# Attention of a hybrid decoder layer: straight-line code, four relayout transfers in place of sixteen, and q loaded ahead of them

## The chip, the cores and the metric

One core of one Trainium2 chip runs the whole kernel. The time is device microseconds (us) of one execution, and less is better. Besides the timed runs there is one profiled execution, with its own time and its own span (from its first to its last instruction).

## The reference

One hybrid layer on 2048 tokens of width 1024. A projection makes q, k, v, a gate and the inputs of a state-space scan; the attention merges three dilated patterns (window 128 step 1, window 512 step 4, window 2048 step 16), normalised by their common denominator, and is gated; the state-space branch is scanned in chunks; both go through one output projection.

```python
u = rms_norm(hid, norm_pre_w)
proj = jnp.einsum('bsd,de->bse', u, w_in)
q, k, v, g_attn, z, xbc, dt_raw = jnp.split(proj, ...)
attn = mixture_of_dilations(q * 64 ** -0.5, k, v)    # 16 heads of 64, 3 patterns, merged by denominators
attn = attn * silu(g_attn)
...                                                   # conv, ssd_chunked, gated group norm: y
out = jnp.einsum('bse,ed->bsd', concat([attn, y]), w_out)
return hid + rms_norm(out, norm_post_w)
```

## The kernel before, in words

The kernel has three blocks in a row: `project` (to about 1260 us), `attend` (to about 1923 us) and `scan_and_project` (to the end). The change touches `attend` alone.

**Work of a head.** The tokens fall into 4 classes by their number modulo 4. A head is 32 units. Units 0 to 15 are "class" units: unit s holds the queries of class c = s % 4 in block n = s // 4, against blocks 0 to n of the same class (this covers the patterns with steps 4 and 16). Units 16 to 31 are "natural" units: 128 tokens in a row against the block before and their own. Two heads are a pair, and the 64 units of a pair are the steps p of one `body`.

**Order of a unit, written out by hand.** TensorE (PE) makes the scores (L1104, L1105: high and rest part of k) three steps ahead; VectorE (DVE) adds the mask and takes the row minimum (L935, from PSUM to `masked`); ScalarE (ACT) exponentiates (L1051); PE transposes the probabilities (L1112); DVE, or at every fourth unit ACT, copies them out (L981, L1087); PE multiplies them with v (L1125) two steps later; ACT reads a group of 8 units out of PSUM (L1063) into `cls_out` (class units) or `nat_out` (natural ones). The rings are four `masked`, `probs` and `probs_t` buffers, three score banks and two banks of transposes, so a stop of one engine reaches the others within a few units.

**Between heads.** `cls_out` of a head has a class unit's 128 queries on the partitions, so SyncE (SP) moves it by DMA into natural order, `cls_nat` (`relayout`, L751: 16 transfers a head, each 32 partitions of source and 4 units of 66 numbers). At unit 3 of the next head DVE takes the common minimum (`merge_drops`, L946, L949), ACT the weights, DVE at unit 5 the denominators and scales (`merge_scales`, L957 to L965). GpSimd (POOL) multiplies and adds the two parts (`merge`, L717, L722); PE transposes a finished pair at units 16, 20, 24 and 28 of an even head (L1136), and DVE gates it. For the last head DVE does the merge too.

**Loads.** SP's queue runs, for head h (`load_head`): wait until head h-2 is weighed with v; 4 + 4 transfers of v for head h (L761, L764); the relayout of head h-1, after a wait for its class groups; then q and k of head h+1 (`load_qk`, L739, two transfers each, after waits that the buffers `raw_q` and `raw_k` are free, which POOL signals with its steps L702 and L704 on head h); for every second head the gate g. Of q and k of the next head ACT takes the high parts at units 5, 7, 9, 11 (q) and 13 to 19 (k), L1030; POOL takes the rests (L702, L704) and sorts q by class (L709). The first score of the next head, made at unit 29, waits for all of it.

**Loops.** On every engine pair 0 and pair 7 are written out and pairs 1 to 6 are one hardware loop, so each engine branches back five times:

```python
            body(0)
            with eng.Fori(1, HEADS // 2 - 1) as pair:
                body(pair)
            body(HEADS // 2 - 1)
```

Of the kernel before, what the change touches and what calls it, by code (L numbers as in the profile page):

```python
# [14 lines left out]
P = 128  # L15
# [496 lines left out]
def attend(nc, dram, dt_bias, a_log, cum_tok, dt_tok):  # L512
# [5 lines left out]
    with ExitStack() as ctx:  # L518
# [25 lines left out]
        cls_out = [sb(f"cls_out{b}", [P, CLASS_UNITS, WIDE]) for b in range(2)]  # L544
        cls_nat = [sb(f"cls_nat{b}", [P, TT, WIDE]) for b in range(2)]
# [36 lines left out]
        pool_waited = sem("pool_waited")  # L582
# [19 lines left out]
        dve_waited = sem("dve_waited")  # L602
# [11 lines left out]
        class Unit:  # L614


            def __init__(self, p):
                self.b, self.s = divmod(p, UNITS)
                self.group = self.s // GROUP
                if self.s < CLASS_UNITS:  # L620
# [6 lines left out]
                    self.min = cls_out[self.b][:, self.s, HEAD_DIM + 1:HEAD_DIM + 2]  # L627
                    self.sum = cls_out[self.b][:, self.s, HEAD_DIM:HEAD_DIM + 1]
# [23 lines left out]
        def loop_pairs(eng, body):  # L652


            body(0)
            with eng.Fori(1, HEADS // 2 - 1) as pair:
                body(pair)
            body(HEADS // 2 - 1)
# [52 lines left out]

        def merge(eng, head, b):
# [3 lines left out]
            for j, (dst, src) in enumerate(((part_a, nat_out[b][:, :, :]), (part_b, cls_nat[b][:, :, 0:HEAD_DIM]))):  # L716
                eng.tensor_tensor(dst[:, :, :], src, scale[:, j, :].unsqueeze(2).broadcast_to([P, TT, HEAD_DIM]),  # L717
                                  ALU.mult).then_inc(merge_part, 1)
# [8 lines left out]
        with nc.Block() as block:  # L727
            @block.sync
            def _(sp):
# [4 lines left out]
                def load_qk(head):  # L734

                    for x, at in (("q", 0), ("k", D_ATTN)):
                        wait(sp, split[x], head)
# [4 lines left out]
                def relayout(head, b):  # L742
# [6 lines left out]
                    for c in range(CLASSES):  # L749
                        for j in range(CLASSES):  # L750
                            sp.dma_start(cls_nat[b][c:P:CLASSES, j:TT:CLASSES, :],  # L751
                                         cls_out[b][j * rows:(j + 1) * rows, c:CLASS_UNITS:CLASSES, :])\
                              .then_inc(relaid, 16)

                def load_head(head, b, is_last=False):
# [7 lines left out]
                    for c in range(CLASSES):  # L763
                        sp.dma_start(v_nat[b][c * SHARE:(c + 1) * SHARE, :, :], v_natural[c][:, :, cols])\  # L764
                          .then_inc(v_in[b], 16)
                    if not is_int(head, 0):
                        relayout(head - 1, 1 - b)
                    if not is_last:
                        load_qk(head + 1)
# [11 lines left out]
                with sp.Fori(1, HEADS // 2 - 1) as pair:  # L781
# [13 lines left out]
            def _(pool):  # L795
# [23 lines left out]
                def head_turn(head, b, has_before=True, has_next=True):  # L819
# [3 lines left out]
                    if has_next:  # L823
# [5 lines left out]
                        for x in "qk":  # L829
                            pool.wait_ge(high_made[x], (head + 2) * TB)  # L830
                            take_rest(pool, x, 1 - b)
                            if x == "q":
                                pool.wait_ge(split[x], head + 2)
                                pool.sem_inc(pool_waited, 1)
# [919 lines left out]
```

## Time and profile before

| what | value |
|---|---|
| median of 3 runs | 2480.7 us |
| lowest and highest run | 2478.7 and 2482.16 us |
| the profiled execution, its own time | 2473.88 us |
| its span | 2472.2 us |
| busy share of the span: PE, PE weight loads, DVE, ACT, POOL | 93%, 80%, 43%, 34%, 29% |
| mean granted TensorE clock (share of full speed) | 0.963 |
| relayout transfers | 256 of 33.0 KB, median 2.0 us from issue to landing |
| transfers of q, and of k | 32 and 32 of 512.0 KB, median 6.2 and 9.6 us |

PE is TensorE's multiplications, PEld its weight loads, SPq the DMA issues of SyncE. In a row of the time line come the start, the duration, the engine, the line, the operation with the tiles it writes and reads, and in brackets the idle time of the engine just before the row and what ended it; "issue" there means that the engine waited for nothing the profile shows. Two heads take about 80 us in the middle of the attention.

### The profile page before, as it was taken

The numbers are of one execution on the slowest core, as the hardware profiler recorded it, in microseconds if no ns is written. First come the engines' busy times: TensorE is split into PE (matmuls) and PEld (weight loads), VectorE is DVE, ScalarE is ACT, GpSimd is POOL, SyncE is SP. The second block draws the span as 40 slices with busy tenths as digits, with TensorE's granted clock in tenths as the row PEclk, the third lists the DMA queues.
The fourth block names the chain that finished last, engine by engine and source line by source line (L and its number), as shares of the span: only waits on it lengthen the run. The fifth ranks groups of instructions, "written<-read, shape, count | busy, mean of one in ns | idle before, by whom it ended". The sixth has DMA issues, their size and how long they took to land. (4 is left out here: it accounts for less than half of the span.)

```text
span 2472.2 us, 36119 instructions
## 1 busy us (share of the span) xinstructions
PE 2306.9 (93%) x12565; PEld 1972.9 (80%) x12565; DVE 1052.8 (43%) x2245; ACT 832.4 (34%) x2013; POOL 709.7 (29%) x348
## 2 busy tenths in 40 slices
PE   6899999999999999999958998998898499999998
PEld 5788888888888888888848988898898278888886
DVE  4200000011111223465556766666577576666661
ACT  5211111111111111221236766676676332222222
POOL 0011111010011100111105544453553345555552
PEclk9999999999999999999979998998999589999999
DMA  4222221121322122122363635544462724444431
GB/s 129 93 77 77 77 76 60 52 76 51 94 76 60 52 76 77 51 76 68 95 123 83 152 79 136 137 113 100 112 151 56 281 94 140 139 139 132 134 109 52
DMA packets 270854, 244.47 MB, mean 99 GB/s; under 512 B 112677, under 2 KB 245985, under 8 KB 259073
## 3 DMA queue, kind: packets, MB, share of 16 engines
q1 hardware_dynamic: 269632, 235.56, 34.3%
q0 software_dynamic: 1104, 7.47, 0.8%
q8 instruction: 58, 0.95, 0.2%
q14 instruction: 60, 0.48, 0.1%
HBM read 160.67 MB, written 73.66 MB: 95 GB/s over the span
## 5 line engine op out<-in xcount | busy, mean ns | idle before, releaser
L442 PE MATMUL mm<-u_hi,w_hi 128*128 128x512 f32 x1696 | 666.4, 393 | 16.2 <-DVE u_lo L371 14.2
L444 PE MATMUL mm<-u_hi,w_lo 128*128 128x512 f32 x1696 | 662.6, 391 | 0.0
L443 PE MATMUL mm<-u_lo,w_hi 128*128 128x512 f32 x1696 | 662.6, 391 | 0.0
L254 POOL TENSOR_TENSOR w_lo<-w_raw,w_hi 128x1024 fp32r<-128x1024 f32 x53 | 139.5, 2632 | 1089.7 <-ACT w_hi L268 1089.7
L442 PEld LDWEIGHTS mm<-u_hi,w_hi 128*128 128x128 f32 x1696 | 320.0, 189 | 84.1 <-DVE u_lo L371 17.3
L444 PEld LDWEIGHTS mm<-u_hi,w_lo 128*128 128x128 f32 x1696 | 319.8, 189 | 66.9
L443 PEld LDWEIGHTS mm<-u_lo,w_hi 128*128 128x128 f32 x1696 | 320.3, 189 | 65.5
L417 DVE COPY tok_tile<-turn 128x512 f32<-128x512 f32 x104 | 64.6, 683 | 578.7 <-PE turn L457 576.5
L1112 PE MATMUL ps_t<-ident_b,probs 128*128 128x128 f32 x1136 | 222.0, 286 | 52.7 <-DVE probs_t L981 38.9
L1639 PE MATMUL ps_out<-wo_hi,mix_hi 128*128 128x512 f32 x512 | 208.0, 406 | 1.3 <-ACT mix_hi L1588 1.3
L1112 PEld LDWEIGHTS ps_t<-ident_b,probs 128*128 128x128 f32 x1136 | 141.6, 145 | 78.6 <-DVE probs_t L981 33.7
L1640 PE MATMUL ps_out<-wo_lo,mix_hi 128*128 128x512 f32 x512 | 200.6, 392 | 0.0
L1125 PE MATMUL ps_o<-v_cls,probs_t 128*128 128x64 f32 x1280 | 182.8, 276 | 0.0
L981 DVE COPY probs_t<-ps_t 128x256 f32<-128x256 f32 (+3 forms) x384 | 171.9, 448 | 22.6 <-issue 19.6
L1125 PEld LDWEIGHTS ps_o<-v_cls,probs_t 128*128 128x128 f32 x1280 | 175.7, 204 | 0.8 <-issue 0.7
L386 DVE SCALAR_TENSOR_TENSOR fm<-half_tanh,mm 128x512 f32<-128x512 f32 x64 | 44.0, 688 | 297.4 <-ACT half_tanh L293 297.4
L935 DVE CUSTOM_DVE_ANT_0 masked<-ps_s,class_mask 128x128 f32<-128x128 f32 (+3 forms) x256 | 124.2, 490 | 91.0 <-PE ps_s L1105 33.9
L1051 ACT ACTIVATE probs<-masked,cls_out 128x128 f32<-128x128 f32 (+3 forms) x256 | 141.7, 556 | 39.0 <-DVE cls_out L935 38.7
L935 DVE CUSTOM_DVE_ANT_0 masked<-ps_s,near_mask 128x256 f32<-128x256 f32 (+1 forms) x256 | 106.3, 415 | 89.6 <-PE ps_s L1105 70.3
L293 ACT ACTIVATE half_tanh<-mm 128x512 f32<-128x512 f32 x64 | 38.2, 597 | 307.2 <-PE mm L444 307.2
L1125 PE MATMUL ps_o<-v_nat,probs_t 128*128 128x64 f32 x992 | 138.7, 261 | 0.0
L1051 ACT ACTIVATE probs<-masked,nat_min 128x256 f32<-128x256 f32 (+1 forms) x256 | 126.3, 497 | 18.5 <-DVE nat_min L935 18.4
(181 smaller groups left out, 3434.0 us busy)
## 6 DMA issues: line engine op xcount, KB each, us to landing
feat<-fm SPq DMA_DIRECT2D x28, 1024.0 KB, 4.7
w_raw<-in_w_in_dram SPq DMA_DIRECT2D x52, 512.0 KB, 6.2
tok<-tok_tile SPq DMA_DIRECT2D x26, 1024.0 KB, 5.6
raw_q<-feat SPq DMA_DIRECT2D x32, 512.0 KB, 6.2
raw_k<-feat SPq DMA_DIRECT2D x32, 512.0 KB, 9.6
cum_b<-cum_scratch SPq DMA_DIRECT2D x16, 1024.0 KB, 7.6
cls_nat<-cls_out SPq DMA_DIRECT2D x256, 33.0 KB, 2.0
tok_tile<-in_x_dram SPq DMA_DIRECT2D x16, 512.0 KB, 3.6
```

The costliest lines, as they stand in the source:

```text
L254: pool.tensor_tensor(w_lo[b][:, :, :], w_raw[b][:, :, :], w_hi[b][:, :, :].bitcast(F32), ALU.subtract).then_inc(w_lo_made[b], 1)
L417: dve.tensor_copy(tok[:, q * 4:q * 4 + 4, :].rearrange("p a b -> p (a b)"), turn[q][:, :])\
L442: pe.matmul(mm[tb][:, :], w_hi[b][:, k, :], u_hi[:, k, block_cols(tb)], start=(k == 0), stop=False)
L443: pe.matmul(mm[tb][:, :], w_hi[b][:, k, :], u_lo[:, k, block_cols(tb)], start=False, stop=False)
L444: last = pe.matmul(mm[tb][:, :], w_lo[b][:, k, :], u_hi[:, k, block_cols(tb)], start=False, stop=(k == KT - 1))
L935: dve.tensor_tensor_reduce(out=masked[p % RING][:, 0:u.width], in0=ps_s[p % S_BANKS][:, 0:u.width], in1=u.mask, scale=1.0, scalar=3e38, op ...
L981: copy_probs(dve, pair, p, lambda o, i: dve.tensor_copy(o, i))
L1051: act.activation(probs[p % RING][:, 0:u.width], masked[p % RING][:, 0:u.width], ACT.Exp, bias=u.min, scale=-1.0, accum_out=u.sum).then_inc ...
L1112: last = pe.transpose(ps_t[p % 2][:, j * P:(j + 1) * P], probs[p % RING][:, j * P:(j + 1) * P], ident[:, :])
L1125: last = pe.matmul(ps_o[u.group % 2][:, (u.s % GROUP) * HEAD_DIM:(u.s % GROUP + 1) * HEAD_DIM], probs_t[p % RING][:, j * P:(j + 1) * P], u ...
L1639: pe.matmul(ps_out[h][:, :], mix_hi[:, kk, :], wo_hi[:, kk, cols_h], start=(kk == 0), stop=False)
L1640: pe.matmul(ps_out[h][:, :], mix_hi[:, kk, :], wo_lo[:, kk, cols_h], start=False, stop=False)
```

## The change

`attend` is written out: `loop_pairs` calls the body for each of the 8 pairs, and the loops of SP and POOL become Python loops too. Semaphore values and addresses become constants, and two counters that nothing waits for (`dve_waited`, `pool_waited`) go. `cls_out` and `cls_nat` are kept as [class, block, 66], so the 4 blocks of a class lie side by side in a partition, and `relayout` is 4 transfers a head of 1056 bytes for each of 128 destination partitions; before it was 16 with pieces of 264 bytes. The readers and writers of the two tiles get other access patterns. In SP's queue q of head h+1 is loaded ahead of the relayout of head h-1, k behind it as before.

```diff
         count, near = masked[2], masked[3]
-        cls_out = [sb(f"cls_out{b}", [P, CLASS_UNITS, WIDE]) for b in range(2)]
-        cls_nat = [sb(f"cls_nat{b}", [P, TT, WIDE]) for b in range(2)]
+        cls_out = [sb(f"cls_out{b}", [P, CLASSES, CLASS_BLOCKS, WIDE]) for b in range(2)]
+        cls_nat = [sb(f"cls_nat{b}", [P, CLASSES, CLASS_BLOCKS, WIDE]) for b in range(2)]
         nat_out = [sb(f"nat_out{b}", [P, TT, HEAD_DIM]) for b in range(2)]
...
                     self.v = [v_cls[self.b][:, c * CLASS_BLOCKS + j, :] for j in range(self.blocks)]
-                    self.min = cls_out[self.b][:, self.s, HEAD_DIM + 1:HEAD_DIM + 2]
-                    self.sum = cls_out[self.b][:, self.s, HEAD_DIM:HEAD_DIM + 1]
+                    self.min = cls_out[self.b][:, c, n, HEAD_DIM + 1:HEAD_DIM + 2]
+                    self.sum = cls_out[self.b][:, c, n, HEAD_DIM:HEAD_DIM + 1]
                 else:
...
-        def loop_pairs(eng, body):
-
-
-            body(0)
-            with eng.Fori(1, HEADS // 2 - 1) as pair:
+        def loop_pairs(body):
+
+
+            for pair in range(HEADS // 2):
                 body(pair)
-            body(HEADS // 2 - 1)
...
+        def by_row(ap):
+
+            return ap.rearrange("p (n j) -> p n j", j=CLASSES)
+
+        def in_order(ap):
+
+            return ap.rearrange("p j n -> p n j")
+
         def merge(eng, head, b):
...
             wait(eng, merge_part, head * 3)
-            for j, (dst, src) in enumerate(((part_a, nat_out[b][:, :, :]), (part_b, cls_nat[b][:, :, 0:HEAD_DIM]))):
-                eng.tensor_tensor(dst[:, :, :], src, scale[:, j, :].unsqueeze(2).broadcast_to([P, TT, HEAD_DIM]),
-                                  ALU.mult).then_inc(merge_part, 1)
+            eng.tensor_tensor(part_a[:, :, :], nat_out[b][:, :, :],
+                              scale[:, 0, :].unsqueeze(2).broadcast_to([P, TT, HEAD_DIM]), ALU.mult).then_inc(merge_part, 1)
+            eng.tensor_tensor(part_b[:, :, :].rearrange("p (n j) f -> p n j f", j=CLASSES),
+                              cls_nat[b][:, :, :, 0:HEAD_DIM].rearrange("p j n f -> p n j f"),
+                              by_row(scale[:, 1, :]).unsqueeze(3).broadcast_to([P, CLASS_BLOCKS, CLASSES, HEAD_DIM]),
+                              ALU.mult).then_inc(merge_part, 1)
             eng.wait_ge(merge_part, head * 3 + 2)
...
-                def load_qk(head):
+                def load_qk(head, which="qk"):
                     for x, at in (("q", 0), ("k", D_ATTN)):
+                        if x not in which:
+                            continue
                         wait(sp, split[x], head)
...
                     rows = P // CLASSES
-                    for c in range(CLASSES):
-                        for j in range(CLASSES):
-                            sp.dma_start(cls_nat[b][c:P:CLASSES, j:TT:CLASSES, :],
-                                         cls_out[b][j * rows:(j + 1) * rows, c:CLASS_UNITS:CLASSES, :])\
-                              .then_inc(relaid, 16)
+                    for j in range(CLASSES):
+                        sp.dma_start(cls_nat[b][:, j, :, :].rearrange("p n f -> p (n f)"),
+                                     cls_out[b][j * rows:(j + 1) * rows, :, :, :].rearrange("p c n f -> p c (n f)"))\
+                          .then_inc(relaid, 16)
...
                           .then_inc(v_in[b], 16)
+                    if not is_last:
+                        load_qk(head + 1, "q")
                     if not is_int(head, 0):
...
                     if not is_last:
-                        load_qk(head + 1)
+                        load_qk(head + 1, "k")
                     if b == 1:
...
                 load_head(1, 1)
-                with sp.Fori(1, HEADS // 2 - 1) as pair:
+                for pair in range(1, HEADS // 2 - 1):
                     load_head(pair * 2, 0)
...
                 head_turn(1, 1)
-                with pool.Fori(1, HEADS // 2 - 1) as pair:
+                for pair in range(1, HEADS // 2 - 1):
                     head_turn(pair * 2, 0)
...
                         wait(dve, scales_made, pair * 2 + u.b - 1)
-                    dve.sem_inc(dve_waited, 1)
                     dve.tensor_tensor_reduce(out=masked[p % RING][:, 0:u.width], in0=ps_s[p % S_BANKS][:, 0:u.width],
...
-                    mins = [nat_min[b][:, :], cls_nat[b][:, :, HEAD_DIM + 1]]
+                    mins = [nat_min[b][:, :], in_order(cls_nat[b][:, :, :, HEAD_DIM + 1])]
                     at = head * 9
-                    dve.wait_ge(relaid, (head + 1) * CLASSES * CLASSES * 16)
+                    dve.wait_ge(relaid, (head + 1) * CLASSES * 16)
                     dve.wait_ge(group_out, head * 4 + 4)
                     dve.wait_ge(exped, head * UNITS + UNITS)
-                    dve.tensor_tensor(both_min[:, :], mins[0], mins[1], ALU.min).then_inc(merge_step, 1)
+                    dve.tensor_tensor(by_row(both_min[:, :]), by_row(mins[0]), mins[1], ALU.min).then_inc(merge_step, 1)
                     dve.wait_ge(merge_step, at + 1)
                     for j in range(2):
-                        dve.tensor_tensor(drop[:, j, :], mins[j], both_min[:, :], ALU.subtract).then_inc(merge_step, 1)
+                        dve.tensor_tensor(by_row(drop[:, j, :]), by_row(mins[j]) if j == 0 else mins[j],
+                                          by_row(both_min[:, :]), ALU.subtract).then_inc(merge_step, 1)
...
-                    sums = [nat_sum[b][:, :], cls_nat[b][:, :, HEAD_DIM]]
+                    sums = [nat_sum[b][:, :], in_order(cls_nat[b][:, :, :, HEAD_DIM])]
                     at = head * 9
...
                     for j in range(2):
-                        dve.tensor_tensor(part_sum[:, j, :], sums[j], weight[:, j, :], ALU.mult).then_inc(merge_step, 1)
+                        dve.tensor_tensor(by_row(part_sum[:, j, :]), by_row(sums[j]) if j == 0 else sums[j],
+                                          by_row(weight[:, j, :]), ALU.mult).then_inc(merge_step, 1)
                     dve.wait_ge(merge_step, at + 5)
...
-                loop_pairs(dve, body)
+                loop_pairs(body)
                 merge_drops(HEADS - 1, 1)
...
                     at = (u.group % 2) * GROUP
-                    dst = (cls_out[u.b][:, at:at + GROUP, 0:HEAD_DIM] if u.s < CLASS_UNITS
-                           else nat_out[u.b][:, at:at + GROUP, :])
+                    if u.s < CLASS_UNITS:
+                        rows = slice(at // CLASSES, (at + GROUP) // CLASSES)
+                        dst = cls_out[u.b][:, :, rows, 0:HEAD_DIM].rearrange("p c n f -> p n c f")
+                        src = ps_o[u.group % 2][:, :].rearrange("p (n c f) -> p n c f", c=CLASSES, f=HEAD_DIM)
+                    else:
+                        dst = nat_out[u.b][:, at:at + GROUP, :]
+                        src = ps_o[u.group % 2][:, :].rearrange("p (u f) -> p u f", f=HEAD_DIM)
                     if u.group == 2:
                         wait(act, merge_part, (pair * 2 + u.b - 1) * 3)
-                    act.activation(dst, ps_o[u.group % 2][:, :].rearrange("p (u f) -> p u f", f=HEAD_DIM), ACT.Copy)\
-                       .then_inc(group_out, 1)
+                    act.activation(dst, src, ACT.Copy).then_inc(group_out, 1)
...
-                loop_pairs(act, body)
+                loop_pairs(body)
                 group_read(HEADS // 2 - 1, STEPS - 1)
...
                 pe.wait_ge(made, 7)
-                loop_pairs(pe, body)
+                loop_pairs(body)
                 for p in range(STEPS - 2, STEPS):
```

## Rows read from the trace of the kernel before

**Rows 1.** Waits, 1334 to 1911 us: total, times, longest (us)

```profile
PE ps_t L1112 <- DVE probs_t L981: 30.5, 10, 4.3
...
DVE masked L935 <- issue: 24.3, 7, 5.2
...
DVE probs_t L981 <- issue: 19.6, 5, 4.5
```

**Rows 2.** Time line of DVE: first step of the merge, at unit 3

```profile
1334.25 0.18 DVE L946 TENSOR_TENSOR both_min<-nat_min,cls_nat 128x16 f32<-128x16 f32 x1
...
1370.04 0.18 DVE L946 TENSOR_TENSOR both_min<-nat_min,cls_nat 128x16 f32<-128x16 f32 x1
...
1406.64 0.17 DVE L946 TENSOR_TENSOR both_min<-nat_min,cls_nat 128x16 f32<-128x16 f32 x1
...
1808.19 0.18 DVE L946 TENSOR_TENSOR both_min<-nat_min,cls_nat 128x16 f32<-128x16 f32 x1
...
1842.48 0.18 DVE L946 TENSOR_TENSOR both_min<-nat_min,cls_nat 128x16 f32<-128x16 f32 x1
...
1879.14 0.18 DVE L946 TENSOR_TENSOR both_min<-nat_min,cls_nat 128x16 f32<-128x16 f32 x1
```

**Rows 3.** Time line of DVE at one backward branch

```profile
1521.74 0.29 DVE L935 CUSTOM_DVE_ANT_0 masked<-ps_s,class_mask 128x128 f32<-128x128 f32 x1 [5.23 <-issue]
...
1529.32 0.42 DVE L981 COPY probs_t<-ps_t 128x256 f32<-128x256 f32 x1 [3.69 <-issue]
```

**Rows 4.** Windows of 10 us: busy (instructions) of PE, PEld, DVE, ACT, POOL; clock; DMA share

```profile
1410.00:1420.00 10.00, 9.59 (x77) 9.03 (x78) 7.77 (x24) 8.89 (x25) 9.36 (x4) 1.00 1.11 316
...
1520.00:1530.00 10.00, 5.79 (x23) 5.02 (x24) 3.62 (x18) 3.99 (x14) 0.00 (x0) 0.62 0.99 194
...
1530.00:1540.00 10.00, 10.00 (x56) 9.20 (x55) 6.54 (x25) 6.20 (x17) 6.13 (x3) 0.70 0.20 41
```

**Rows 5.** DMA queues of kind instruction, 1366 to 1438 us: packets, MB

```profile
q8 instruction: 5, 0.08, 0.5%
...
q14 instruction: 6, 0.05, 0.3%
```

**Rows 6.** Time line of PE: idle after the wait for q

```profile
1338.96 0.44 PE L1112 MATMUL ps_t<-ident_b,probs 128*128 128x128 f32 x2 [1.77 <-ACT probs L1051]
...
1374.32 0.44 PE L1112 MATMUL ps_t<-ident_b,probs 128*128 128x128 f32 x2 [1.34 <-ACT probs L1051]
...
1811.51 0.44 PE L1112 MATMUL ps_t<-ident_b,probs 128*128 128x128 f32 x2 [0.31 <-ACT probs L1051]
...
1846.96 0.44 PE L1112 MATMUL ps_t<-ident_b,probs 128*128 128x128 f32 x2 [1.56 <-ACT probs L1051]
```

**Rows 7.** Time line of ACT: the wait for q ahead of one of them

```profile
1373.15 0.63 ACT L1030 ACTIVATE q_parts<-raw_q 128x512 fp32r<-128x512 f32 x1 [1.85 <-DMA raw_q<-feat]
```

**Rows 8.** Time line of SP's DMA issues ahead of it

```profile
1355.14 10.49 SPq L751 DMA_DIRECT2D cls_nat<-cls_out  x16
...
1365.91 1.20 SPq L739 DMA_DIRECT2D raw_q<-feat  x2
```

**Rows 9.** Time line of POOL in the same stretch

```profile
1345.40 4.54 POOL L702 TENSOR_TENSOR q_parts<-raw_q,q_parts 64x2048 fp32r<-64x2048 f32 x1 [1.50 <-ACT q_parts L1030]
...
1356.19 4.54 POOL L704 TENSOR_TENSOR k_rest<-raw_k,k_high 128x2048 fp32r<-128x2048 f32 x1 [2.12 <-ACT k_high L1030]
```

**Rows 10.** Groups by form, 1334 to 1911 us: merge and group read

```profile
L717 POOL TENSOR_TENSOR part_b<-cls_nat,scale 128x1024 f32<-128x1024 f32 x15 | 28.5, 1902 | 0.0
...
L717 POOL TENSOR_TENSOR part_a<-nat_out,scale 128x1024 f32<-128x1024 f32 x15 | 28.5, 1898 | 186.8 <-DVEq L967 186.8
...
L1063 ACT ACTIVATE cls_out<-ps_o 128x512 f32<-128x512 f32 x30 | 17.8, 595 | 0.0
```

**Rows 11.** Time line at the last merge: DVE

```profile
1911.11 0.19 DVE L946 TENSOR_TENSOR both_min<-nat_min,cls_nat 128x16 f32<-128x16 f32 x1 [2.41 <-DMA cls_nat<-cls_out]
```

**Rows 12.** The same stretch: ACT, the last group read

```profile
1909.57 0.60 ACT L1063 ACTIVATE nat_out<-ps_o 128x512 f32<-128x512 f32 x1 [1.52 <-PE ps_o L1125]
```

More of the change, by code:

```diff
@@ L581, in attend @@
         q_sorted = sem("q_sorted")
-        pool_waited = sem("pool_waited")
         v_in = [sem(f"v_in{b}") for b in range(2)]
@@ L601, in attend @@
         last_out = sem("last_out")
-        dve_waited = sem("dve_waited")
         dt_in = sem("dt_in")
@@ L833, in head_turn @@
                                 pool.wait_ge(split[x], head + 2)
-                                pool.sem_inc(pool_waited, 1)
                                 sort_q(pool, 1 - b)
```

## The prediction, made before the changed kernel was run

> **What bounds the kernel now.** I read the waits of the attention stretch first, then the time line of DVE and of PE, then windows of 10 us. PE is busy nearly all the time in this kernel, so what counts is where PE stands still or runs at a lower clock. Between 1334 and 1911 us PE has one large wait, for DVE's copy of the probabilities: 30.5 us in ten times [rows 1]. DVE itself was then waiting for nothing but its instructions: 24.3 us ahead of the mask and 19.6 us ahead of the copy. Ten of these twelve waits come in pairs, one pair at each of the five backward branches; the other two are 0.2 and 0.5 us. One such place: 5.23 us before the mask, and 7.6 us later 3.69 us before the copy [rows 3]. The windows show what comes with it: 23 and then 56 multiplications in 10 us instead of the 77 of an undisturbed busy stretch, and a granted clock of 0.62 and 0.70, that is part of the time at the lower of its two levels, after PE had been idle; elsewhere it is 1.00 [rows 4].
>
> To price it I use a landmark: DVE's first step of the merge, at unit 3 of each head [rows 2]. Between two of them lies one head. Intervals without a branch are 35.79 and 34.29 us (the work of an odd head), and 36.60 and 36.66 us (an even head, with the 16 transposes of a finished pair). Each has one more idle time of PE, of 1.77, 0.31, 1.34 and 1.56 us [rows 6]: ACT waits at unit 5 for q of the next head, 1.85 us in the second of them [rows 7], and so falls behind with the exponentials. Taken off, the clean heads are 34.02 and 33.98, 35.26 and 35.10 us: 34.0 + 35.2 = **69.2 us for a pair**. That written-out and looped heads agree within 0.2 us says that register arithmetic and the counters cost nothing; it is only the branch.
>
> **The change, part by part.**
>
> (a) The five backward branches go. From the landmark at 1406.64 to that at 1808.19 are 401.55 us for ten heads with all five branches [rows 2]. Clean they are 5 x 69.2 = 346.0. The difference is **55.5 us**: 30.5 us of PE's idle time [rows 1], the rest the low clock behind it and the waits for q of these heads. It is all on the path, since PE is. A price for written-out code in its place: the first pass through the loop, 1366 to 1438 us, had to bring in its instructions like any written-out code, 5 and 6 transfers on the two instruction queues [rows 5], and DVE shows no wait of more than 0.2 us for them there. The transfers of other data do not hold them up either: from 1410 to 1420 us the DMA share is 1.11 and PE is 9.59 of 10 us busy at full clock [rows 4]. So I take 0, with 5.5 us (55.5 / 10) per transfer as the upper end, which is what an exposed one costs today.
>
> (b) q ahead of the relayout. Before: SP issues sixteen relayout transfers from 1355.14 on, q at 1365.91 [rows 8], and q has landed at 1373.15 [rows 7], 7.2 us later. The new order adds a wait of SP, for the buffer of q, ahead of the relayout, k and g. It ends when POOL has taken the rest of q, at 1345.40 + 4.54 = 1349.9 [rows 9]; the relayout was released only at 1355.1, so it is not held up. q lands at about 1357.2, and ACT wants it at 1373.15 - 1.85 = 1371.3: the wait goes, with 14 us to spare. Outside the branches this gives 1.77 + 1.34 + 0.31 + 1.56 = **5.0 us** [rows 6]; the waits inside the branch stretch are in (a) already. Next in line behind q is nothing large: k needs its buffer, free at 1356.19 + 4.54 = 1360.7 [rows 9], and is then issued 6 us earlier than before (1367.3), for use some units later than q. The v transfers that follow keep their own wait (the head before last weighed) and start where they did.
>
> (c) The relayout, 4 for 16. An issue cost SP 10.49 / 16 = 0.66 us for 33 KB, and 0.60 us for half of raw_q with 512 KB [rows 8], so the time goes by the transfer and not by its bytes: 4 x 0.66 = 2.6 us instead of 10.5. Upper end: unchanged 10.5. For fifteen heads it is hidden, since the merge that reads `cls_nat` comes at unit 3 of the next head. After the last head it is not: DVE waited 2.41 us for the last transfer, until 1911.11 [rows 11]. That wait goes, but the same instruction also waits for the last group read of ACT, which ends at 1909.57 + 0.60 = 1910.2 [rows 12]. So the gain is **0.9 us**, not 2.4; lower end 0.
>
> (d) Access patterns. POOL's product takes 1.902 us from `cls_nat` with its gaps and 1.898 us from `nat_out` without any [rows 10]: steps cost nothing there. With one dimension more I take the same; twice as long would be 1.9 us a head, against the 2.12 us that POOL waits for ACT before the rest of k [rows 9], so it is covered. ACT's group read is 0.595 us [rows 10]; twice that for two groups a head would be 1.2 us and up to 19 us over 16 heads if none were covered. I take 0, because its output went already in rows of 64 with gaps of 2 between them. DVE's small merge steps are 0.18 to 0.19 us [rows 11]; 0 as well.
>
> **Sum.** 55.5 + 5.0 + 0.9 = 61.4 us. Against the profiled execution's own 2473.9 us that is 2412.5 us. The median of the runs is 6.8 us above that execution, and nothing in the change touches this difference: 2480.7 - 61.4 = **2419.3 us**, which I forecast.
>
> **The rivals.**
>
> *Only the first wait of each pair goes* (the second, ahead of the copy, stays in some form). For it: it comes 7.6 us behind the branch, not at its target. Then 19.6 / (23.7 + 19.6) = 45% of the 55.5 us stays, 25 us: 2444 us. Against it: no such wait stands in any written-out stretch or in the loop's first pass, which ran the same instructions in the same place. Chance 0.05. The Trainium skill, page "Runtime: NRT & Kernel Launch", section "Instruction fetch mechanics", says that fetching runs ahead sequentially, that crossing to the next block is mostly hidden and that a taken branch breaks it. By that rule the first wait is the fetch and the second would need another cause, which is this rival. The trace agrees with the rule on the first and speaks against it on the second, 3.69 us.
>
> *The early q gives nothing*: ACT's stop at unit 5 has another cause, or q's buffer is not free in time. Mean of the four idle times is 1.25 us, in 14 heads 17.4 us: 2437 us. For it: 1.34 us of idle PE is less than the 1.85 us of the wait, so PE's idle time need not follow it one for one. Against: 14 us of slack. Chance 0.08.
>
> *The waits are not the branch's* but come from the load on the DMA queues at that moment (share 0.99 in the window [rows 4]), so the written-out code has them too; then only q and the end gain: 2480.7 - 18.3 = 2462 us. Against it the window with 1.11. Chance 0.02.
>
> *Slower: written-out code does not get its instructions in time.* The six middle pairs then bring in about 11 transfers each [rows 5] that the loop brought in fewer times. With 5.5 us for an exposed one the gain is used up at 61.4 / 5.5 = 11 of some 66. If five in each pair were exposed, 30 x 5.5 = 165 us: 2584 us. The place is DVE, the engine that already shows such waits. Against it: pair 0, the first pass and pair 7. Chance 0.03.
>
> **How the numbers follow.** Main case 0.82. Its own range is about 10 us to either side: 7 us because the profiled execution differs that much from the median, 3 us for the terms. Upward the range takes in the second rival: 2409 to 2440 us, which holds 0.90. About 0.2% (5 us) is what a measurement can tell from no change; the cases faster than that have 0.97 in sum, less 0.01 for one that meets exposed fetches by halves: faster 0.96, same 0.01, slower 0.03.
>
> **What would show it.** In the changed profile the landmarks must stand 34 and 35.2 us apart throughout; the rows "masked <- issue" and "probs_t <- issue" of DVE must be gone, and with them PE's wait for the copy; the clock must be 1.00 in the windows between 1340 and 1850 us. ACT must no longer wait for raw_q, and raw_q must be issued ahead of the relayout by several us. The last merge must wait for the group read and no DMA. Intervals of 38 us or more with waits for "issue" would prove the fetch rivals; 35.3 and 36.5 us with a wait of ACT would prove the second.

## The result and the profile after

The changed kernel takes **2406.7 us** (median of 4 runs, 2405.9 to 2407.7) beside 2479.7 us for the kernel before, measured with it: ratio 0.9703, 95% interval 0.9688 to 0.9717. The forecast was 2419.3 us in a range from 2409 to 2440 us, so the gain of 73 us is 12 us larger than forecast and 2 us outside the range.

From the profile page of the changed kernel: busy time and share, the clock row of the 40 slices, the two instruction queues, the relayout's transfers:

```profile
span 2405.4 us, 34104 instructions
PE 2279.1 (95%) x12565; PEld 1952.9 (81%) x12565; DVE 1053.1 (44%) x2245; ACT 827.1 (34%) x2013; POOL 708.1 (29%) x348
...
PEclk9999999999999999999996999999998599999999
...
q8 instruction: 82, 1.34, 0.2%
q14 instruction: 55, 0.45, 0.1%
...
cls_nat<-cls_out SPq DMA_DIRECT2D x64, 132.0 KB, 2.7
```

The engines do the same work. PE is busy for 28 us less with as many multiplications, since fewer of them run at the low clock (the transposes' mean fell from 286 to 278 ns). One instruction queue moved 82 transfers where it had 58, the other 55 where it had 60; the relayout's transfers of 132 KB land in 2.7 us.

The waits between 1334 and 1845 us, largest of PE, DVE and ACT, answer to [rows 1]:

```profile
ACT probs_t L1101 <- PE ps_t L1126: 104.6, 105, 2.1
DVE masked L943 <- PE ps_s L1119: 103.1, 235, 1.1
...
ACT probs L1061 <- DVE cls_out L943: 8.0, 30, 0.7
...
PE ps_t L1126 <- ACT probs L1061: 4.3, 14, 0.3
DVE masked L943 <- ACT probs L1061: 4.0, 16, 0.3
```

PE's 30.5 us behind DVE, DVE's 43.9 us for "issue" and ACT's waits for q are gone, and the mean granted clock of that stretch is 1.00 (columns as in [rows 4]):

```profile
1334.00:1844.00 510.00, 503.49 (x4242) 485.53 (x4240) 380.80 (x1465) 388.86 (x1255) 279.57 (x94) 1.00 0.54 129
```

The landmark of [rows 2], five times and the last:

```profile
1333.28 0.17 DVE L954 TENSOR_TENSOR both_min<-nat_min,cls_nat 128x16 f32<-128x16 f32 x1
1366.85 0.17 DVE L954 TENSOR_TENSOR both_min<-nat_min,cls_nat 128x16 f32<-128x16 f32 x1
1401.75 0.18 DVE L954 TENSOR_TENSOR both_min<-nat_min,cls_nat 128x16 f32<-128x16 f32 x1
1435.31 0.17 DVE L954 TENSOR_TENSOR both_min<-nat_min,cls_nat 128x16 f32<-128x16 f32 x1
...
1812.53 0.18 DVE L954 TENSOR_TENSOR both_min<-nat_min,cls_nat 128x16 f32<-128x16 f32 x1
1843.74 0.19 DVE L954 TENSOR_TENSOR both_min<-nat_min,cls_nat 128x16 f32<-128x16 f32 x1 [1.55 <-ACT nat_out L1078]
```

Every head but the last lasts 33.56 or 34.90 us, a pair 68.5 us where I had 69.2. The last merge waits for the group read, as forecast for (c). From the first landmark to the last are 510.5 us; before, 576.9 us.

Seen from this trace alone, the forecast looks nearly right: every mark that it named is there. The experiments show that its main step was wrong all the same.

### The profile page after: what moved, and what is told of

Read it like the earlier page. It is cut to its first block and busy times, and to the rows that moved or that the text cites. A ratio compares the mean times of both kernels' runs of the same rounds, so it can differ in the third digit from the quotient of the medians.

```text
span 2405.4 us, 34104 instructions
## 1 busy us (share of the span) xinstructions
PE 2279.1 (95%) x12565; PEld 1952.9 (81%) x12565; DVE 1053.1 (44%) x2245; ACT 827.1 (34%) x2013; POOL 708.1 (29%) x348
## 5 line engine op out<-in xcount | busy, mean ns | idle before, releaser
L1126 PE MATMUL ps_t<-ident_b,probs 128*128 128x128 f32 x1136 | 214.2, 278 | 13.8 <-DVE probs_t L991 7.9
L1139 PE MATMUL ps_o<-v_cls,probs_t 128*128 128x64 f32 x1280 | 174.1, 268 | 0.0
L1139 PEld LDWEIGHTS ps_o<-v_cls,probs_t 128*128 128x128 f32 x1280 | 166.4, 195 | 0.0
L1061 ACT ACTIVATE probs<-masked,cls_out 128x128 f32<-128x128 f32 (+3 forms) x256 | 141.5, 555 | 13.1 <-DVE cls_out L943 13.1
L289 ACT ACTIVATE fm<-mm 128x512 f32<-128x512 f32 x64 | 38.3, 599 | 273.8 <-PE mm L444 273.8
```

The costliest lines, as they stand in the source:

```text
L1061: act.activation(probs[p % RING][:, 0:u.width], masked[p % RING][:, 0:u.width], ACT.Exp, bias=u.min, scale=-1.0, accum_out=u.sum).then_inc ...
L1126: last = pe.transpose(ps_t[p % 2][:, j * P:(j + 1) * P], probs[p % RING][:, j * P:(j + 1) * P], ident[:, :])
L1139: last = pe.matmul(ps_o[u.group % 2][:, (u.s % GROUP) * HEAD_DIM:(u.s % GROUP + 1) * HEAD_DIM], probs_t[p % RING][:, j * P:(j + 1) * P], u ...
```

## The experiments

### The kernel before, again

No edit; it is here for a second profiled execution.

> The kernel of before, unchanged, for a second profiled execution and more times. Theory A (the median of before lies 6 us above its profiled execution because its ten waits for instructions differ from execution to execution): the profiled span and DVE's waits for issue move together; a span near 2479 us comes with about 5 us more of such waits and of low clock than the 24.3 + 19.6 us of the first profile, a span near 2472 us with the same. Theory B (the difference lies elsewhere, in the projection or the scan): DVE's waits for issue and the length of the attention are as in the first profile whatever the span, and another block is longer.

Measured: 2480.6 us (10 runs, 2470.9 to 2489.4), ratio 1.0007 (0.9989 to 1.0025); the profiled execution took 2479.15 us, 5.3 us more than the first. Its waits:

```profile
PE ps_t L1112 <- DVE probs_t L981: 30.1, 10, 4.3
DVE masked L935 <- issue: 23.9, 7, 5.2
DVE probs_t L981 <- issue: 19.3, 5, 4.3
PE ps_t L1112 <- ACT probs L1051: 15.3, 31, 2.9
...
ACT q_parts L1030 <- DMA raw_q<-feat: 14.7, 9, 3.4
```

and PE after the first late q:

```profile
1339.63 0.44 PE L1112 MATMUL ps_t<-ident_b,probs 128*128 128x128 f32 x2 [2.90 <-ACT probs L1051]
```

DVE's waits for instructions are those of the first profile (43.2 against 43.9 us), so theory A is false in its cause: what differs is how late q comes, 2.90 us of idle PE in this head where [rows 6] have 1.77. The clock is lower behind it, too: from 1339 to 1350 us the granted clock is 0.84 here and 1.00 in the first profile, and this head takes 38.5 us instead of 35.8. The attention took 582.9 us between the landmarks instead of 576.9. Theory B is false too, the other blocks did not lengthen. The kernel before scatters over 18 us, the changed one over 2 (and over 4 in its repetition below).

### Written out, nothing else

```diff
-            body(0)
-            with eng.Fori(1, HEADS // 2 - 1) as pair:
+            for pair in range(HEADS // 2):
                 body(pair)
-            body(HEADS // 2 - 1)
```

(and the same for the loops of SP and POOL)

> The kernel of before with the loops written out and nothing else: sixteen relayout transfers, q behind them. Theory A: the branch is most of the gain; the wait of ACT for q is back in all 14 heads with 1.25 us of idle PE and some tenths behind it, and the last merge waits for its transfer again: 2406.7 + 14 x 1.4 + 0.9 = 2427 us (2422 to 2432), no wait of DVE for issue. Theory B (the new layout gives several us by itself, beyond the wait for q): above 2435 us.

Measured: 2457.2 us (2451.6 to 2465.8), ratio 0.9922 (0.9892 to 0.9953). Only 22 us. Its waits:

```profile
ACT q_parts L1028 <- DMA raw_q<-feat: 31.9, 14, 3.7
PE ps_t L1110 <- ACT probs L1049: 29.0, 28, 3.2
```

DVE's waits for "issue" are gone but for 0.8 us. In their place every head waits for q: 31.9 us in fourteen, against 13.9 us in ten between 1334 and 1911 us before. The stop at the branch had given q the time to land: four of the five heads with a branch did not wait for q at all before, and here they do. Without the stop the next unit 5 comes sooner, and q, issued behind sixteen relayout transfers, does not: one q is issued at 1510.94 us and ACT can begin on it only at 1518.99. How much of these 8 us comes from sharing the DMA engines with k and v no run shows. The clock was lower too: of the 55 windows of 10 us from 1340 to 1890 us, 11 lie below 1.00, the lowest at 0.66. The number is on theory B's side (above 2435 us), but not by B's cause, the layout: the run "Written out, q ahead of sixteen transfers" below keeps the old layout and takes 2411.1 us. The wait for q is A's mechanism, with a price of its own that A had too low.

### The loops back in the changed kernel

The reverse edit on all five engines, with the two counters; new layout, four transfers and early q stay.

> The changed kernel with the hardware loops and the two counters put back on all engines; four relayout transfers and early q stay. Theory A: five branches at 10.5 to 12.5 us each, without any wait for q: 2406.7 + 57 = 2464 us (2457 to 2470); DVE waits for issue in pairs at five places. Theory B (the waits came from SP's long row of transfers at the same moment, which is shorter now): the waits shrink below half, under 2435 us.

Measured: 2427.8 us (2425.3 to 2429.8), ratio 0.9798 (0.9781 to 0.9814). So the loops cost 21 us here, not 57: theory B's side. Two of DVE's five branches:

```profile
1437.91 0.29 DVE L949 CUSTOM_DVE_ANT_0 masked<-ps_s,class_mask 128x128 f32<-128x128 f32 x1 [2.99 <-issue]
1509.47 0.29 DVE L949 CUSTOM_DVE_ANT_0 masked<-ps_s,class_mask 128x128 f32<-128x128 f32 x1 [2.69 <-issue]
```

One wait of 2.7 to 3.0 us per branch; no second one. And the stretch around the second, in windows (columns as in [rows 4]):

```profile
1500.00:1510.00 10.00, 8.34 (x72) 7.91 (x71) 5.20 (x25) 5.41 (x20) 0.52 (x1) 1.00 0.50 116
1510.00:1520.00 10.00, 9.63 (x68) 8.31 (x69) 8.52 (x37) 8.61 (x28) 4.43 (x3) 1.00 0.54 96
```

PE stands still for 1.7 to 2.0 us at each branch and its granted clock stays at 1.00 in these windows; in [rows 4], behind 4.27 and 1.87 us of idle PE, it was 0.62.

### q behind the four transfers

```diff
-                    if not is_last:
-                        load_qk(head + 1, "q")
                     if not is_int(head, 0):
                         relayout(head - 1, 1 - b)
                     if not is_last:
-                        load_qk(head + 1, "k")
+                        load_qk(head + 1)
```

> The changed kernel with q loaded behind the relayout again, together with k. Theory A (the two edits do the same thing: four transfers end 8 us earlier, so q, issued behind them, is there in time anyway): 2406.7 us within 2 us, no wait of ACT for raw_q. Theory B (q has to go ahead of the relayout): the waits of ACT at unit 5 are back, 2406.7 + 14 x 1.4 = 2426 us; half of that if q is late by less.

Measured: 2404.1 us (2403.1 to 2405.3), heads of 33.56 and 34.89 us, no wait for raw_q. The median is 2.6 us below the changed kernel's, slightly more than theory A allowed; in the repetition below the difference is gone. Theory A: in written-out code four transfers make the early q unnecessary.

### The loops with one of the two SP edits at a time

The first (`loops_early_q`) is the kernel of before with q loaded ahead of its sixteen transfers; the second (`loops_four`) is the changed kernel with the loops back and q behind the four. Their diffs are those of the two sections above and this one:

```diff
+                    if not is_last:
+                        load_qk(head + 1, "q")
                     if not is_int(head, 0):
                         relayout(head - 1, 1 - b)
                     if not is_last:
-                        load_qk(head + 1)
+                        load_qk(head + 1, "k")
```

> The kernel of before (loops, sixteen relayout transfers) with q alone loaded ahead of the relayout. Theory C (new: a fetch at a branch takes as long as the data transfers in flight let it; before, q and k, 2 MB, were issued 1.5 to 3 us ahead of DVE's branch, after the sixteen relayout transfers): half of the 2 MB is gone from that moment, so the first wait falls from 5.1 to about 4 us, the second shrinks or goes, and no head waits for q: 2445 us (2435 to 2455). Theory D (only q's lateness costs, the branch has its fixed price): DVE's waits stay at 5.1 and 3.7 us, time 2479 - 14 x 1.4 = 2460 us or more.

> The changed kernel with the loops back and q loaded behind the four relayout transfers, with k. Theory C: q and k are issued 8 us earlier than before, 8 to 9 us ahead of the branch, and have landed by then: within 4 us of the kernel with loops and early q (2427.8 us), first wait 2.7 to 3.3 us, no second. Theory D: same first number but DVE's waits unchanged, 2460 us.

Measured: 2445.5 us (2445.2 to 2450.2), ratio 0.9852 (0.9821 to 0.9882), and 2443.6 us (2437.9 to 2443.8), ratio 0.9831 (0.9799 to 0.9862). In each half or more of the way to 2427.8 us. The branches in `loops_early_q`, the first and the second of five:

```profile
1436.41 0.29 DVE L939 CUSTOM_DVE_ANT_0 masked<-ps_s,class_mask 128x128 f32<-128x128 f32 x1 [2.92 <-issue]
1442.54 0.42 DVE L985 COPY probs_t<-ps_t 128x256 f32<-128x256 f32 x1 [2.73 <-issue]
1515.32 0.29 DVE L939 CUSTOM_DVE_ANT_0 masked<-ps_s,class_mask 128x128 f32<-128x128 f32 x1 [4.86 <-issue]
```

and SP's issues ahead of the third of these rows, and of the 4.25 us in `loops_four`:

```profile
1509.27 1.17 SPq L741 DMA_DIRECT2D raw_k<-feat  x2
```

```profile
1500.00 1.18 SPq L752 DMA_DIRECT2D raw_q<-feat  x2
1502.93 1.11 SPq L752 DMA_DIRECT2D raw_k<-feat  x2
```

The branch is taken to be where the wait begins: 1515.32 - 4.86 = 1510.5, 1.2 us after k was issued. In `loops_four` it is 1513.28 - 4.25 = 1509.0, 6 us after k. I had expected waits of about 4 us in `loops_early_q` and of 2.7 to 3.3 us in `loops_four` and got mostly 4.8 to 5.0 us and 3.7 to 4.9 us: one load of 1 MB, issued 1.2 us ahead, lengthens the first wait nearly as much as two do. The second wait is gone (but for one, 2.73 us), and no head waits for q. For `loops_early_q` theory C holds in time (2445 us forecast) and in kind. For `loops_four` it missed the time by 16 us: I had forecast 2427.8 us within 4 us, because I took q and k to have landed by the branch. They had not: the last packets of these loads start at about 1511.0 us, 2 us behind the branch. Theory D, unchanged waits and 2460 us, falls in both.

### v moved away from the branch

In `loops_back` the v transfers start about 1.5 us after the branch. Here, in the same kernel, they go behind q and the relayout, and k, behind them, comes last.

```diff
+                    if not is_last:
+                        load_qk(head + 1, "q")
+                    if not is_int(head, 0):
+                        relayout(head - 1, 1 - b)
                     wait(sp, weighed, (head - 1) * UNITS)
                     cols = bass.ds(head * HEAD_DIM + V_COL, HEAD_DIM)
...
                           .then_inc(v_in[b], 16)
                     if not is_last:
-                        load_qk(head + 1, "q")
-                    if not is_int(head, 0):
-                        relayout(head - 1, 1 - b)
-                    if not is_last:
                         load_qk(head + 1, "k")
```

> The changed kernel with the loops back, and each head's eight v transfers issued behind the relayout of the head before instead of right at the branch, so that q's load, the relayout, v and k come in the middle of a head. Theory C: if the v transfers, which start at the branch, are what is left of the load, DVE's wait falls below 2.5 us and the time lies 3 to 8 us under the 2427.8 us of the loops. Theory F (2.7 us is a fetch with nothing in its way): waits of 2.7 us as before, 2427.8 us within 3 us.

Measured: 2446.1 us (2445.5 to 2447.9), ratio 0.9850 (0.9821 to 0.9879), 18 us slower than `loops_back`. Neither theory. SP's row and DVE's branch behind it:

```profile
1504.71 2.26 SPq L777 DMA_DIRECT2D v_cls<-tok  x4
1507.06 2.06 SPq L780 DMA_DIRECT2D v_nat<-tok  x4
1509.32 1.18 SPq L752 DMA_DIRECT2D raw_k<-feat  x2
```

```profile
1518.29 0.29 DVE L949 CUSTOM_DVE_ANT_0 masked<-ps_s,class_mask 128x128 f32<-128x128 f32 x1 [4.52 <-issue]
```

The edit brought v, 1 MB in eight transfers, ahead of the branch and k nearer to it: v is issued from 9 us ahead on, k 4.5 us ahead (1518.29 - 4.52 = 1513.8) instead of 6.1. The waits are 4.1 to 4.8 us instead of 2.7 to 3.0, with the same instructions, the same loops and the same layout; only the order of SP's queue differs. Put together from the time lines of DVE and SP, with the branch taken to be where the wait begins, and from the packets of instruction queue q14 in the same traces:

| kernel | loads issued ahead of the branch (us ahead) | first wait at its five branches, us | of it, until the instruction packet starts, us | second waits |
|---|---|---|---|---|
| `loops_back`: four, q ahead | k 6.1 | 2.99, 2.69, 2.71, 2.76, 2.71 | 0.6 to 0.7 | none |
| `loops_four`: four, q behind | q 9.0, k 6.1 | 4.93, 4.25, 4.38, 3.99, 3.65 | 1.1 to 2.3 | none |
| `loops_v_later`: v moved | v from 9.0 on, k 3.9 to 4.6 | 4.68, 4.52, 4.11, 4.66, 4.84 | 1.7 to 2.5 | none |
| `loops_early_q`: sixteen, q ahead | k 0.2; then k 1.2 | 2.92; 4.86, 4.91, 4.84, 4.98 | 0.6; 2.2 to 2.4 | 2.73 at the first |
| before: sixteen, q behind | q at the branch; then q 1.1, k 0.3 behind it | 3.13; 5.23, 5.05, 5.12, 5.12 | 0.8; 2.4 to 2.6 | 3.7 to 4.5 at all |

The packets show that these stops are fetches. In each of the 31 stops of the table exactly one packet of q14 starts, and from its start to the end of the stop it is always 2.1 to 2.7 us. What makes a stop long is the time before the packet starts, and that follows the loads: in the kernel with v moved the packet starts at 1515.9 us, and the last packets of the loads start between 1515.5 and 1516.5; with k issued 1.2 us ahead, or q 1.1 us ahead and k just behind, it starts 2.2 to 2.6 us into the stop. So a fetch at a branch takes as long as the loads in flight let it. The second stops are fetches too: in the kernel of before the next packet starts 8 us behind the first and inside the second stop, while in `loops_back` it starts 2.6 to 3.1 us behind the first and no second stop comes.

Where a load is issued only at the branch itself (the first branch in the last two rows) the first wait is short and the next fetch is caught instead.

With v moved PE was idle for 3.2 to 3.9 us at each branch, 3.56 us at this one, and the clock fell:

```profile
1510.00:1520.00 10.00, 6.44 (x50) 6.00 (x51) 3.90 (x20) 4.11 (x17) 0.00 (x0) 0.92 0.60 128
1520.00:1530.00 10.00, 10.00 (x61) 9.47 (x60) 7.66 (x30) 6.94 (x23) 4.53 (x3) 0.74 0.00 1
```

From the first to the last landmark it is 545.6 us instead of 527.4 in `loops_back`, so the attention alone is 18 us longer. The first landmark also came 3.4 us later, at 1338.1 us, since the v transfers of the first head start at 1277.2 us instead of 1266.9, behind the q of the next; in the profiled execution that comes on top (2445.9 against 2425.3 us).

### Written out, q ahead of sixteen transfers

The kernel written out alone, with the diff of `loops_early_q`.

> Written-out code with q ahead of sixteen relayout transfers in the old layout. Theory C (the written-out kernel with q behind them stood at 2457 us only because q came late): no wait for raw_q, k is late enough for its first use by ten units: 2407 to 2411 us. Theory E (SP's long row of transfers itself disturbs, or k is late next): above 2415 us, with a wait of ACT for raw_k or of PE for k_rest.

Measured: 2411.1 us (2410.2 to 2411.4), ratio 0.9708 (0.9679 to 0.9736), no wait for raw_q or raw_k: theory C. Against `written_out_only` this single edit of SP's order is worth 46 us (43 us of it between the landmarks, 557.2 against 514.0).

### The changed kernel again, and q behind four again

No new edit; the two were run beside each other on one chip.

> The changed kernel, unchanged, beside the next three on one chip. Theory G (the 2.6 us between it, 2406.7, and the kernel without early q, 2404.05, lie between chips or placements, since the heads of both last 33.56 and 34.9 us): here both within 1 us of each other. Theory H (early q costs something): 2 to 3 us apart again.

> The changed kernel with q behind the four relayout transfers, again, beside the changed kernel on one chip. Theory G: equal within 1 us. Theory H: 2 to 3 us less than the changed kernel.

Measured side by side: 2404.8 us (2403.1 to 2406.8) and 2405.4 us (2403.4 to 2406.3), ratios 0.9698 and 0.9700. Theory G; the early q neither costs nor gives with four transfers. The 2.6 us of before lay outside the attention, whose heads are the same to 0.02 us.

### The counters back

```diff
                         wait(dve, scales_made, pair * 2 + u.b - 1)
+                    dve.sem_inc(dve_waited, 1)
                     dve.tensor_tensor_reduce(...)
```

> The changed kernel with the two counters that nothing waits for put back (one increment of DVE ahead of each of the 512 mask operations, sixteen of POOL's); otherwise written out, four transfers, early q. Theory I (the counters are what makes heads of 33.80 and 34.95 us with the old layout into 33.56 and 34.90 us, since DVE's waits for ACT ahead of the mask fell from 26.6 to 4.0 us): heads of 33.8 and 34.95 us, 7 x 0.3 = 2 us more. Theory J (it was the layout): heads as in the changed kernel.

Measured: 2408.8 us (2406.2 to 2412.2). Heads of 33.80 and 34.95 us, and two of DVE's rows:

```profile
DVE masked L947 <- ACT probs L1065: 27.5, 79, 0.6
...
ACT probs L1065 <- DVE cls_out L947: 13.6, 30, 1.0
```

Theory I: from first to last landmark 513.0 us instead of 510.2, so 2.8 us are the increments (the 512 ahead of the mask, with POOL's sixteen put back too), more than the 2 us expected; three of the seven even heads took 35.1 to 35.3 us. The other 1.3 us of the medians are within the scatter of the runs.

### Written out on DVE alone

The changed kernel with the counters and with the loops on ACT, PE, SP and POOL as before, on DVE none; for ACT, and PE likewise:

```diff
-                loop_pairs(body)
+                looped_pairs(act, body)
```

> The changed kernel with the loops on PE, ACT, SP and POOL, written out on DVE alone (with the counters). Theory K (DVE's branch is the only one on the path; ACT's and PE's bodies come back without a wait): the changed kernel's time plus 2 to 4 us for the counters and register arithmetic, no head over 35.4 us. Theory L (another engine's branch stands behind DVE's): heads with a branch 1 to 2 us longer, 2415 us or more, with a wait for issue on ACT or PE.

Measured: 2411.1 us (2410.4 to 2413.4). Heads of 33.80 and 35.17 us, one of 35.5; no wait for issue on ACT or PE above 0.6 us. Theory K in kind; the time is 6.4 us above the changed kernel's 2404.8 instead of 2 to 4, and one head exceeds its 35.4 us. Against `counters_back` the medians differ by 2.3 us and the landmarks by 1.3 (514.3 against 513.0), so the branches of the other four engines and their register arithmetic cost 1 to 2 us together. Against `loops_back` DVE's five branches make the attention 527.4 - 514.3 = 13.1 us longer, 2.6 us each.

## Why the prediction was right or wrong

All four orders of SP's queue, with loops and written out (medians in us; DVE's waits for issue with loops in brackets, from each kernel's waits between 1334 us and the end of its attention):

| | sixteen, q behind | sixteen, q ahead | four, q behind | four, q ahead |
|---|---|---|---|---|
| loops | 2479.7 (44) | 2445.5 (26) | 2443.6 (22) | 2427.8 (14.5) |
| written out | 2457.2 | 2411.1 | 2404.1, 2405.4 | 2406.7, 2404.8 |

The two written-out kernels with four transfers were each run twice. The loops cost 22, 34, 39 and 22 us; SP's two edits together give 52 us with loops and 51 us written out. The parts do not add, because each stop hides another. In the last column the loops make 17.2 us between the landmarks (527.4 against 510.2): 13.1 for DVE's branches, 1.3 for the other engines, 2.8 for the counters; the rest of the 22 lies in other blocks and in scatter.

**Reading and landmark.** Right: PE sets the pace, DVE's branch stops it, ACT's wait for q does so beside it. The direction and the disappearance of every marked row came as forecast.

**Step (a), the step that failed:** "55.5 us ... all on the path" as the price of the branch. It is the price of the branch with 2 MB of q and k issued within 1.5 us of it. With the changed order of SP's queue the same five branches cost 13 us on DVE and 1 to 2 us on the rest, and with the old order taking them away gave 22 us, since q was then late. About two thirds of what I booked under the loops (55.5 less 15 to 22 us) belongs to SP's edits. I had this as a rival, "the waits are not the branch's", and gave it 0.02, with the window at 1410 us against it (DMA share 1.11, no wait). That window proves nothing of a branch: DVE waits for no fetch there, so how long one takes under load does not show. The rival was also put as all or nothing, while the truth is a product: no branch, no wait; load, a wait nearly twice as long (5.2 against 2.7 us) with a second behind it. My first rival, by which the second wait needs a cause other than a fetch, falls as well: an instruction packet starts inside each second wait. "Runtime: NRT & Kernel Launch" of the Trainium skill, section "Instruction fetch mechanics", says that a taken branch stalls for a DMA fetch where its target is not in what is already loaded. DVE's traces agree, with one instruction packet in each stop; the size of one such stop here, 2.7 to 5.2 us by what else is in flight, came only from these runs. Why ACT and PE show no such stop at their branches stays open.

**Step (b), mis-sized:** the wait for q was priced from the four heads outside the branches, 5.0 us, and 17.4 us if all fourteen had it. Taken away alone, in written-out code, it is worth 46 us (2457.2 to 2411.1). Its measured size in the trace of before was small because the branch stops had covered it, and because the four idle times of PE, 0.3 to 1.8 us, came without a low clock, while in `written_out_only` they reach 3.2 us, 29.0 us in all, with windows down to 0.66 behind them. The timing in (b) was right: q is issued ahead of the relayout and waited for no more.

**The clean head, mis-sized by 0.7 us a pair** (5.0 us in all). The counters were taken as free, because looped and written-out heads agreed; but both had them. They cost 0.24 us in an odd and 0.05 us or more in an even head, 2.8 us in all. Most of the rest is how the rows of PE are to be read: idle time counts from the modelled end of a multiplication, while an undisturbed one would start 0.1 to 0.2 us before that end, so each idle row stands for a little more than its figure. This last reading was argued from the rows, not tried.

**The median, 7.2 us.** I carried the 6.8 us between the profiled execution and the median over to the changed kernel, as untouched by the change. The second profile of before, 5.3 us above the first with 6.1 us more in the attention, shows where they lie: q came later there. The kernel of before scattered over 18 us in ten runs. The change took this scatter away, and its profiled execution lies 0.4 us above its median.

**(c) and (d)** held. An issue of the relayout takes 0.65 us with 132 KB (2.61 us for four), as it did with 33 KB, POOL's product from the new layout 1.902 us, the group read 0.594 us, the last merge 0.9 us sooner: the last interval is 31.2 us in the changed kernel and 32.1 us in the written-out kernels with sixteen transfers (31.7 to 32.0 with loops).

The account: 5.0 us in the heads, 7.2 us for the median, 0.4 us at the two ends: 12.6 us, the difference between 2419.3 and 2406.7. These sizes put the number outside the range; the failure of (a) does not show in it. That the sum came out near is luck in one respect: (a) and the rest of (b) were wrong in opposite directions, and since the change makes both edits, the total of the two was what the landmarks gave.

## What to carry to other kernels

A stop that is measured in a trace has its price only together with what it runs beside: before it is booked to one edit of several, ask what its length depends on (here the loads in flight) and what it hides (here a transfer that was late anyway). Large loads do not belong right ahead of a backward branch at which an engine has to fetch: here the two edits of SP's queue, which left one load of 1 MB 6 us ahead of it and also brought q in time, were worth more (52 us) than removing the loop (22 us). What counts seems to be that the load has landed: 2 MB issued 9 and 6 us ahead still cost 3.7 to 4.9 us a branch. Where a median and its profiled execution differ by more than the runs of a quiet kernel do, the scatter may itself be a wait to be found, and a second profile can find it.

## What the runs showed of the hardware that was not expected

- A fetch at DVE's backward branch took 2.7 to 3.0 us with k alone issued 6 us ahead of it and up to 5.2 us, with a second fetch of 3.6 to 4.5 us behind it, when q and k were issued at that moment (table above). Its instruction packet always started 2.1 to 2.7 us before the end of the stop; the loads delayed that start.
- PE and ACT, with bodies of the same 64 steps, showed no such wait at their branches beyond 0.6 us (the run with DVE alone written out).
- In `loops_back` the granted clock stayed at 1.00 when PE was idle for 1.7 to 2.0 us; with v moved it fell to 0.92 and 0.74 in the two windows around 3.56 us. The length of one idle time does not settle it: in `written_out_only` the clock fell behind 1.99 us of idle PE at 1520 us, to 0.66 in the window from 1520 to 1530 us.
- One increment of a semaphore ahead of each of 512 operations of DVE, an engine that was 75% busy in that stretch, with sixteen of POOL's, made the attention 2.8 us longer.
